# A fused two-block transformer kernel: one low-weight step moved ahead of a norm block at each seam, a row scaling moved behind a wide group's first step, and the projections' merge begun per token half

## The reference, cut to what matters

```python
h = fox_attention(rmsnorm(x, norm_g[0]), fox_w_in, fox_b_f, fox_w_out)   # ... @ fox_w_out
x = x + rmsnorm(h, norm_g[1])                                            # first seam
h = sqrelu_mlp(rmsnorm(x, norm_g[2]), mlp_w1, mlp_w2)
x = x + rmsnorm(h, norm_g[3])                                            # second seam
h = rms_norm(x, norm_g_2)
y_a = (att * silu(z_a)) @ w_proj_a
y_b = (sgu * silu(z_b)) @ w_proj_b
merged = sigmoid(g_a) * y_a + sigmoid(g_b) * y_b                         # the merge
return x + merged @ w_out
```

## Time and profile before

| | before |
|---|---|
| median of 3 runs | 1750.6 us |
| the profiled execution's own time | 1751.51 us |
| its span, first to last instruction | 1749.7 us |
| PE busy | 1742.9 us, 100% of the span |
| PE weight loads (PEld) busy | 1479.5 us, 85% |
| DVE busy | 1428.4 us, 82% |
| ACT busy | 956.6 us, 55% |
| POOL busy | 242.2 us, 14% |
| TensorE granted clock | 1.00 of full speed |

### The profile page before, as it was taken

One profiled execution on the slowest core, in us unless ns is written; L12 is line 12 of the kernel. 1 busy time (PEld: TensorE's weight loads), 2 busy tenths in 40 slices (PEclk: granted clock), 3 DMA queues, 4 the chain that ended last, 5 costly groups with the idle time before them and its releaser, 6 DMA issues.

```text
span 1749.7 us, 23934 instructions
## 1 busy us (share of the span) xinstructions
PE 1742.9 (100%) x8698; PEld 1479.5 (85%) x8698; DVE 1428.4 (82%) x1864; ACT 956.6 (55%) x1306; POOL 242.2 (14%) x324
## 2 busy tenths in 40 slices
PE   9999999999999999999999999999999999999999
PEld 7888888888888888888888887888888888888887
DVE  6557777986799779878987887999888899986798
ACT  7434444556556445644654555767655565564453
POOL 1123434001000210111011000010222100001000
PEclk9999999999999999999999999999999999999999
DMA  8776677655767986798679776556566666668656
GB/s 332 229 255 205 202 207 202 198 189 189 225 209 237 247 251 217 233 259 241 212 230 264 232 228 229 192 196 210 197 205 192 183 198 210 208 213 239 201 200 185
DMA packets 123776, 382.67 MB, mean 219 GB/s; under 512 B 14672, under 2 KB 15328, under 8 KB 123296
## 3 DMA queue, kind: packets, MB, share of 16 engines
q1 hardware_dynamic: 102896, 333.24, 56.6%
q0 software_dynamic: 19920, 47.74, 13.3%
q10 hardware_dynamic: 864, 0.44, 0.1%
HBM read 370.85 MB, written 36.19 MB: 233 GB/s over the span
## 4 chain that ended last, share of the span: by engine, by line
PE 96%; DVE 3%; ACT 1%; issue 0%; POOL 0%; DVEq 0%; ACTq 0%; POOLq 0%
PE bank L549 23%; PE bank L570 16%; PE bank L836 13%; PE bank L835 13%; PE bank L834 13%; PE bank L554 12%; PE bank L620 1%; PE bank L586 1%; DVE w_lo L1781 1%; PE bank L699 1%; PE bank L742 1%; PE bank L757 1%; ACT w_hi L1197 0%; PE bank L748 0%; PE bank L741 0%
## 5 line engine op out<-in xcount | busy, mean ns | idle before, releaser
L1781 DVE TENSOR_TENSOR w_lo<-raw,w_hi 128x1024 fp32r<-128x1024 f32 x620 | 748.5, 1225 | 202.7 <-ACT w_hi L1197 200.1
L1197 ACT ACTIVATE w_hi<-raw 128x1024 fp32r<-128x1024 f32 x620 | 646.9, 1054 | 425.8 <-PE bank L554 155.4
L549 PE MATMUL bank<-h_both,w_hi 128*128 128x512 f32 x1792 | 434.7, 395 | 0.0
L549 PEld LDWEIGHTS bank<-h_both,w_hi 128*128 128x128 f32 x1792 | 330.9, 188 | 65.9
L554 PEld LDWEIGHTS bank<-h_both,w_lo 128*128 128x128 f32 x1792 | 229.8, 191 | 8.7
L554 PE MATMUL bank<-h_both,w_lo 128*128 128x256 f32 x1792 | 232.5, 283 | 0.0
L834 PE MATMUL bank<-w_hi,h_both 128*128 128x512 f32 (+1 forms) x382 | 148.2, 388 | 0.0
L836 PE MATMUL bank<-w_lo,h_both 128*128 128x512 f32 (+1 forms) x382 | 147.8, 387 | 0.0
L835 PE MATMUL bank<-w_hi,h_both 128*128 128x512 f32 (+1 forms) x382 | 147.8, 387 | 0.0
L570 PE MATMUL bank<-w_hi,a_both 128*128 128x512 f32 x448 | 138.8, 391 | 0.0
L834 PE MATMUL bank<-w_hi,a_both 128*128 128x512 f32 x320 | 124.6, 389 | 0.2 <-DVE w_lo L1781 0.2
(11 more groups left out here) (342 smaller groups left out, 2509.7 us busy)
## 6 DMA issues: line engine op xcount, KB each, us to landing
raw<-in_stream SPq DMA_DIRECT2D x557, 512.0 KB, 4.3
summed<-in_stream POOLq DMA_DIRECT2D x130, 256.0 KB, 6.1
raw<-in_stream SPq DMA_DIRECT2D x68, 256.0 KB, 3.1
raw<-summed SPq DMA_DIRECT2D x65, 256.0 KB, 4.0
wide<-scaled POOLq DMA_DIRECT2D x21, 256.0 KB, 4.5
res<-in_x SPq DMA_DIRECT2D x4, 512.0 KB, 7.2
rowg<-in_norm_rows POOLq DMA_DIRECT2D x2, 1024.0 KB, 8.9
gate<-cum_rows POOLq DMA_DIRECT2D x1, 2048.0 KB, 7.6
```

Source lines behind the costliest of these rows:

```text
L549: pe.matmul(tile_sum[b][:, :], w_hi[:, slot + half, k * P:(k + 1) * P], h_both[:, 8 * half + k, :], start=half == 0 and k == 0, stop=False)
L1197: nc.scalar.activation(w_hi[:, slot, :], raw[:, slot, :], ACT.Copy).then_inc(hi_ready, 1)
L1781: nc.vector.tensor_tensor(w_lo[:, slot, :], raw[:, slot, :], w_hi[:, slot, :].bitcast(F32), ALU.subtract).then_inc(lo_ready, 1)
```

## The change

Four pieces of order are changed; no arithmetic is.

1. **Seams.** `next_rest(e + 7)`, the `w_lo` of the seam's fourth chunk, goes ahead of `norm_block(norm, 3)` on DVE. On PE the exception for that chunk and half (lo by hi before hi by lo) is dropped.
2. **Fox row scaling.** The two `fox_gain(0, t)` go from in front of the narrow group's last `next_rest` into the wide group's second step, behind its first `next_rest`. PE's wait for them moves from in front of the first step's `seven_blocks` to in front of its `form_products`. To allow that, the banks of `f_seven` are reordered, so that `seven_blocks` touches banks 4 and 5 and `form_products` banks 3 and 2.
3. **Join.** Since the second of these banks is now bank 5, which `last_group` overwrites, PE waits there for `join_step` 4 (all four join operations) in place of 2.
4. **Merge.** In `proj_a` the two halves are merged one after the other, product then addition, the first on `half_group_done` in place of `chunk_done`.

```diff
--- before.py
+++ after.py
@@ -299,7 +299,7 @@
         group_bank = [bank[2:4], bank[4:6]]
         gate_bank = [bank[2:4], bank[0:2]]
         f_bank = [bank[0], bank[1], bank[6], bank[7]]
-        f_seven = [bank[4], bank[2], bank[5], bank[3]]
+        f_seven = [bank[4], bank[5], bank[2], bank[3]]
         plain_bank = [[bank[6], bank[7], bank[0], bank[1]], bank[2:6]]
         seven_bank = [[bank[2], bank[5], bank[3], bank[4]], plain_bank[0]]
         h_bank = [[bank[2], bank[3], bank[7], bank[6]], [bank[0], bank[1], bank[5], bank[4]]]
@@ -704,16 +704,10 @@
                     pe.wait_ge(xt_hi, 2 * step_count(norm, 4 * t + j) + 2)
                     pe.wait_ge(hi_ready, c + j + 1)
                     products(h_hi, w_hi, j == 0)
-                    if t == 0 and j == 3:
-                        h_in(j)
-                        products(h_lo, w_hi)
-                        pe.wait_ge(lo_ready, c + j + 1)
-                        mm = products(h_hi, w_lo)
-                    else:
-                        pe.wait_ge(lo_ready, c + j + 1)
-                        products(h_hi, w_lo)
-                        h_in(4 * t + j)
-                        mm = products(h_lo, w_hi)
+                    pe.wait_ge(lo_ready, c + j + 1)
+                    products(h_hi, w_lo)
+                    h_in(4 * t + j)
+                    mm = products(h_lo, w_hi)
                     if t == 1:
                         mm.then_inc(chunk_done, 1)
 
@@ -887,6 +881,8 @@
                     return [part[:, f, :] for part in (forms.w_hi, forms.w_lo)]
 
                 pe.wait_ge(form_lo_ready, FIRST_STEP[w] + q + 1)
+                if w == FOX_WIDE and first:
+                    pe.wait_ge(group_taken[0], 4)
                 product(seven[3], x_form(2), w_form(1), first, last)
                 if late:
                     late()
@@ -928,7 +924,6 @@
             def fox_group():
 
                 def before_seven(j):
-                    pe.wait_ge(group_taken[0], 4)
                     pe.wait_ge(group_taken[1], 3)
                     pe.wait_ge(att_ready, FOX_HEADS)
 
@@ -940,7 +935,7 @@
                            lambda j, pair: None, before_seven, {})
 
             fox_group()
-            joined(FOX_WIDE)
+            fifth_read(FOX_WIDE)()
             last_group(FIRST["fox_out"] + 24, 2, 1, a_hi, a_lo,
                        before={4: lambda: pe.wait_ge(join_step, 8 * FOX_WIDE + 8)})
 
@@ -2053,8 +2048,8 @@
                 next_rest(e + 6)
                 norm_block(norm, 2)
                 add_res(norm, 3)
+                next_rest(e + 7)
                 norm_block(norm, 3)
-                next_rest(e + 7)
                 add_res(norm, 4)
                 norm_block(norm, 4)
                 norm_block(norm, 5)
@@ -2187,9 +2182,6 @@
                 if j == 7:
                     fox_x(3)
                     input_form_lo(2, 2, fox_forms)
-                    dve.wait_ge(rowg_in, 16)
-                    for t in range(NT):
-                        fox_gain(0, t)
                 next_rest(c + j)
                 if j == 1:
                     dve.wait_ge(bias_ready, 16)
@@ -2204,8 +2196,14 @@
                     fox_x(j - 3)
                 if 5 <= j < 7:
                     input_form_lo(j - 5, j - 5, fox_forms)
+            def fox_gains():
+
+                dve.wait_ge(rowg_in, 16)
+                for t in range(NT):
+                    fox_gain(0, t)
+
             for q in range(STEPS):
-                wide_step(FOX_WIDE, q, fox_forms)
+                wide_step(FOX_WIDE, q, fox_forms, between=fox_gains if q == 1 else None)
                 if q == 1:
                     input_form_lo(3, 3, fox_forms)
             wide_join(FOX_WIDE, f_seven, f_part)
@@ -2611,17 +2609,20 @@
                 if n == 3:
                     h_forms_lo(2, 0)
                     h_forms(2, 1)
-                dve.wait_ge(chunk_done, c + 4 * n + 4)
                 cols_n = slice(n * GROUP_COLS, (n + 1) * GROUP_COLS)
                 if n >= 2:
                     dve.wait_ge(merged_turned, 2 * n - 2)
                 for t in range(NT):
+                    if t == 0:
+                        dve.wait_ge(half_group_done, GROUPS_BEFORE["proj_a"] + n + 1)
+                    else:
+                        dve.wait_ge(chunk_done, c + 4 * n + 4)
                     nc.vector.scalar_tensor_tensor(out=merged[n % 2][:, t, :], in0=gate[:, t, cols_n], scalar=1.0,
                                                    in1=gate_bank[n % 2][t][:, :], op0=ALU.add,
                                                    op1=ALU.mult).then_inc(merge_ready, 1)
-                dve.wait_ge(merge_ready, 2 * n + 10)
-                dve.sem_inc(gate_taken[n % 2], 1)
-                for t in range(NT):
+                    dve.wait_ge(merge_ready, 2 * n + 9 + t)
+                    if t == 1:
+                        dve.sem_inc(gate_taken[n % 2], 1)
                     nc.vector.tensor_tensor(merged[n % 2][:, t, :], merged[n % 2][:, t, :], merge_b[:, t, cols_n],
                                             ALU.add).then_inc(merged_f, 1)
                 next_rest(c + 4 * n + 3)
```

## The result

| | before | changed |
|---|---|---|
| median of the runs, us | 1750.63 (1750.54 to 1751.72, 8 runs) | 1755.94 (1753.58 to 1757.29, 8 runs) |
| ratio, 95% interval | | 1.0028 [1.0019, 1.0037] |
| profiled execution, us (span) | 1751.51 (1749.7) | 1757.29 (1755.5) |
| mean granted clock of the span | 1.0 | 0.998 |

The change is slower, by 5.3 us between the medians. The forecast was 1754.0 us with a range of 1753.1 to 1755.0: the sign of the sum held, its size did not, and the median lies outside the range. The eight runs of the changed kernel spread over 3.7 us, from 1753.58 to 1757.29, and the granted clock goes with them: 1.000 in the two fastest (1753.58 and 1755.01), 0.999 or 0.998 in the other six.

A forecast was written before the change was run, and what follows sets the result against it. PE was taken to bound the kernel, busy 1742.9 of 1749.7 us. Fox scaling 3.27, join 0.0, seams 0.0 and merge 0.1 made +3.4 us on the median 1750.6: 1754.0 us, range 1753.1 to 1755.0.

The forecast's parts named there:

- Fox scaling: Fox wide group, first `form_products`: PE waits for the moved scaling, load 3.81 us late, net +3.27 us.
- old stand: Fox wide group, behind the first step's nine `form_products` matmuls: PE's existing 0.43 us wait for `w_lo` would vanish.
- The margin of 0.3 us at `f_w_lo`: Fox wide group, second step: `f_w_lo` ready at 350.0, PE's load at 350.3, so no second stand.
- What DVE gains from the two instructions taken out: Scaling's old place: 1.40 us of DVE comes free, but the next `w_lo` waits for ACT; nothing gained.
- Seams, join, merge: The three other places: seams 0.0 us each, join 0.0 (at most 0.1), merge +0.1.
- The clock: During PE's 3.4 us without a matmul in the fox group, the clock holds at 2.4 GHz; no added cost.
- The rival "clock falls": Behind the fox stand matmuls run at half rate, adding 2.0 to 2.6 us: 1756.0 to 1756.6; chance 0.06.
- The other two rivals: Fox group: DVE's chain up to 1.4 us earlier, 1752.6 to 1753.5, chance 0.06; wait met in time, 1750.3, 0.04.

The follow-up runs named there:

- filled kernel: Changed kernel with 15 extra matmul calls of zeros on PE ahead of its wait for the scaling: 1753.98 us, ratio 1.0018.
- seams and merge together: Changed kernel with its fox scaling and join pieces undone, leaving the seams' order and the merge by halves: 1750.72 us, ratio 1.0.
- the scaling at the start of the second step: Changed kernel with the fox row scalings moved up to the start of the wide group's second step: 1752.38 us, ratio 1.0011.
- the fox piece alone: Kernel before with only the scaling and its wait moved, banks reordered and join wait raised; no seams or merge: 1756.47 us, ratio 1.0033.
- the longer stand: Changed kernel with the scalings one `w_lo` later, behind the second of the three: 1757.2 us, ratio 1.0038.
- the shorter stand: Changed kernel with the scalings one instruction earlier on DVE, ahead of the second step's first `w_lo`: 1753.9 us, ratio 1.0021.

## Why the prediction was wrong in size

Point by point, by its own steps:

- **Fox scaling.** Right. Stand of the load 3.83 late, forecast 3.81; scaling 1.28, forecast 1.28; release 0.17, forecast 0.15; old stand gone; net 3.29, forecast 3.27. The filled kernel gives 3.55 for the whole change without the clock, forecast 3.4. The margin of 0.3 us at `f_w_lo` held as well: in the filled kernel, at full pace, it ended at 347.63 + 1.76 = 349.39, 0.32 ahead of the load at 349.71, and no second stand came.
- **What DVE gains from the two instructions taken out.** Right: nothing. In the changed kernel its `w_lo` waited 2.46 us for ACT, and started at 332.52, 0.19 earlier than before, as PE's whole program was (0.18).
- **Seams, join, merge.** Right in cost: 0, 0 and 0.04 (forecast 0.1), and 1750.72 against 1750.43 for seams and merge together. The merge's chain took the 2.83 us of the sum (1655.63 to 1658.46); it began 0.08 earlier against PE, where at most 0.03 was allowed. The join's zero held behind the stand; by itself it is 0.1, and 0.2 with the scaling at the start of the second step.
- **The clock.** This is the step that failed. I priced it at nothing by one row, the last window of the span: 4.4 us with no matmul, PEclk 1.00. What it cost was 2.77 us in the profiled execution and 1.8 between the medians, nearly all of the 1.9 by which the forecast was low. That row was one case of one execution. A fall of the clock is not set by the length of the stand alone: counted from the start of the last matmul it fell after 2.9 us in the changed kernel (340.31 to about 343.2), 3.5 in the fox piece alone (340.38 to about 343.9), 4.1 in the longer stand (339.73 to about 343.8), and in the shorter stand, 2.7 long, it fell in five runs of eleven. Right behind the window I had read, before's own clock fell as well: PEclk is 0.88 in the microsecond from 1750 (below), so the fall lies between 4.7 and 5.7 us after its last matmul at 1745.31. The clock fell at the end of every one of the ten profiled executions, after 3.2 us in the fox piece alone (1750.44 to about 1753.6), 3.9 in the seams and merge alone (1745.47 to about 1749.4) and 4.2 to 5.4 in the others; before's (1750.76 in windows of 0.2 us, so 5.45) is the latest of the ten. So the row was at the late end of a spread, and I had read it as if the clock held up to 4.4 each time. Why the moment differs is open; the runs show only that it does.

```profile
1749.00:1750.00 1.00, 0.00 (x0) 0.00 (x0) 0.00 (x0) 0.00 (x0) 0.00 (x0) 1.00 0.00 0
1750.00:1751.00 1.00, 0.00 (x0) 0.00 (x0) 0.00 (x0) 0.00 (x0) 0.00 (x0) 0.88 0.00 0
```

- **The rival "clock falls"** was what happened. It had 0.06, and its condition, "from a stand somewhere near 3.4 us on", was too high an edge, as the 2.7 us show. Its price, 2.0 to 2.6, is close: 2.77 in the changed kernel's profile, 1.52 in the fox piece alone, 1.8 to 2.5 between medians. Its 1756.0 to 1756.6 holds e.g. the run at 1756.08, and the median 1755.94 is just under it. The page whose warning stood in the prediction, the Trainium skill, TensorE: Matmul & The Clock Gate, "Why this matters for your kernels", was right against the row; the runs agree with it, since a gap of this size between bursts took the clock down in 12 of 14 executions.
- **The other two rivals** did not come: DVE did not move up by the 1.40 us taken out (0.19, with PE's 0.18), and the wait was not met.
- **The range.** With the row weighed as one draw and the warning against it, the clock deserved far more than 0.06, and the range should have reached to about 1757; that is said with the result known.

## What to carry over

A stand of PE has two prices. One is its own length, less what the restart and an old stand give back; in these traces it came out within a tenth of a microsecond of what the order of the releasing engine said. The other is the clock's, here 0 to 2.8 us on top of 3.3, which varies from execution to execution. Price it by the runs or as a chance, never by the one window in which it did not happen. Before work that PE waits for is moved behind other work of DVE, look at what PE has to do until then; here it had nothing for 3.4 us, and the cheaper move was the other one, into the idle time ahead.

## What the runs showed beyond that

- The clock's fall has no fixed delay and its spell no fixed length: 5.9 us of matmuls at half rate in the changed kernel (344.17 to about 350.1), 3.2 in the fox piece alone (344.24 to about 347.4), with the same stand ahead, and 5.9 again behind the stand of 5.0 us (344.73 to about 350.6).
- 30 small matmuls (15 calls) of zeros in the stand kept the clock at 1.00 in all eleven runs, and took 1.8 to 2.5 us off the median though they do no work. That remedy doesn't make the change good, as its stand remains.
- At a clock of 1.00 a kernel still spreads by 1 to 2 us. One source shows in the traces: single stands of 0.4 to 0.6 us at the wide groups' weights, in different places in each execution. The changed kernel's profile has one at 691.84; ACT's `w_hi` that it hangs on had waited 1.31 us for a weight transfer:

```profile
689.50 1.06 ACT L1192 ACTIVATE w_hi<-raw 128x1024 fp32r<-128x1024 f32 x1 [1.31 <-DMA raw<-in_stream]
```

```profile
691.84 0.19 PEld L828 LDWEIGHTS bank<-w_hi,a_both 128*128 128x128 f32 x1 [0.41 <-issue]
```

The profile before has no such stand. The one with the seams and the merge alone has two, at 555 and 1027. The traces show two more sources: the first `form_products` of the fox group, ahead of which all versions do nearly the same, is wanted anywhere between 339.73 and 340.50, and from the last matmul's start to the end of the span it is 3.4 us (filled kernel) to 4.4 (before). Whether the three together make up the whole spread was not tried.
